# One stream of expert gathers instead of closed rounds, in a one-core encoder step

## The reference

```
a = rmsnorm(h, norm_mix);  z = a @ w_in
o_a, conv_state, S = gdn_mixer(...)      # causal conv, chunked delta rule; carries conv_state and S to the next tile
o_b, k, v, logf   = fox_mixer(...)       # causal attention over all keys so far
h = h + concat(o_a, o_b) @ w_out
h = h + peer(rmsnorm(h, norm_ffn))       # below
gate = sigmoid(rmsnorm(h, norm_ple) @ w_ple_gate)
h = h + (p @ w_ple_proj) * gate
y = rmsnorm(h, norm_final)

peer(x), per token: 8 heads pick 16 of 16384 experts each (product keys, top-16), 128 picks in all
  e, gate = picks and softmax of their scores
  a   = sum_d peer_u[e] * x              # 128 rows of 1024 gathered from peer_u
  out = sum_k gate * gelu(a) * peer_v[e] # 128 rows of 1024 gathered from peer_v
```

## Time and profile before

| | us |
|---|---|
| median of 3 runs | 4261.04 (4250.48 to 4262.46) |
| profiled execution, its own time | 4246.57 |
| its span | 4244.8 |
| DVE busy | 3223.5 (76%) |
| PE busy | 2874.7 (68%) |
| POOL busy (issuing gathers) | 2510.8 (59%) |
| ACT busy | 812.4 (19%) |

### The profile page before, as it was taken

The page is one execution under the profiler, slowest core; times in us unless marked ns, Lnnn a source line. Parts: engine busy times, 40 slices in busy tenths (PEclk is TensorE's granted clock), DMA queues, the critical chain, the costliest instruction groups (busy, mean ns, idle before and its releaser), DMA issues. The chain is left out here.

```text
span 4244.8 us, 38975 instructions
## 1 busy us (share of the span) xinstructions
PE 2874.7 (68%) x12714; PEld 1947.2 (46%) x12714; DVE 3223.5 (76%) x6384; ACT 812.4 (19%) x1609; POOL 2510.8 (59%) x2213
## 2 busy tenths in 40 slices
PE   6746576875777666766687577877688575756456
PEld 5644353643454344544365345545455434535122
DVE  3477878788877878797878887797868785796764
ACT  2112111221122112321122112221122112211111
POOL 0036765577556755676556756676556654675573
PEclk9878788987889788988899798888898787978778
DMA  5269998999999998999899999999898999999896
GB/s 187 88 252 367 335 378 310 409 364 367 358 369 387 339 395 330 405 353 376 318 409 357 362 364 356 369 343 391 334 411 307 370 345 269 389 350 374 277 388 250
DMA packets 388057, 1454.11 MB, mean 343 GB/s; under 512 B 64528, under 2 KB 67537, under 8 KB 353297
## 3 DMA queue, kind: packets, MB, share of 16 engines
q0 software_dynamic: 313344, 1140.99, 72.1%
q1 hardware_dynamic: 73200, 305.92, 18.6%
q10 hardware_dynamic: 1312, 4.72, 0.3%
HBM read 1441.69 MB, written 9.51 MB: 342 GB/s over the span
## 5 line engine op out<-in xcount | busy, mean ns | idle before, releaser
L487 POOL DMA_INDIRECT ring<-peer_u,idx_c x1061 | 1250.8, 1179 | 764.9 <-DVE dots L1412 393.7
L1000 PE MATMUL bank<-ring,diag 128*128 128x512 f32 x1920 | 1151.1, 738 | 763.5 <-DMA ring<-peer_v,idx_c 699.1
L1412 DVE CUSTOM_DVE_ANT_0 ring<-ring,xn_c 128x1024 f32<-128x1024 f32 x1088 | 1317.0, 1225 | 461.0 <-DMA ring<-peer_u,idx_c 425.4
L487 POOL DMA_INDIRECT ring<-peer_v,idx_c x1088 | 1218.0, 1120 | 666.8 <-PE bank L1000 285.2
L1000 PEld LDWEIGHTS bank<-ring,diag 128*128 128x128 f32 x1920 | 407.0, 229 | 1286.1 <-DMA ring<-peer_v,idx_c 865.3
L1420 DVE SCALAR_TENSOR_TENSOR h_c<-ring,wgt,h_c 128x1024 f32<-128x1024 f32 x608 | 781.6, 1286 | 224.0 <-DMA ring<-peer_v,idx_c 213.1
L764 PEld LDWEIGHTS bank<-aT,wring 128*128 128x128 f32 x4608 | 564.2, 202 | 113.3 <-issue 39.2
L764 PE MATMUL bank<-aT,wring 128*128 128x128 f32 x4608 | 570.4, 286 | 62.2 <-DVE aT L1036 24.5
L768 PE MATMUL bank<-wring,aT 128*128 128x256 f32 (+1 forms) x1440 | 349.1, 400 | 44.7 <-DVEq L1060 27.3
L768 PEld LDWEIGHTS bank<-wring,aT 128*128 128x128 f32 x1440 | 287.3, 202 | 122.8 <-issue 67.7
L720 ACT ACTIVATE diag<-ident,wgt 128x128 f32<-128x128 f32 x480 | 179.0, 393 | 300.1 <-PE bank L1000 234.0
(11 more groups left out here) (272 smaller groups left out, 2949.8 us busy)
## 6 DMA issues: line engine op xcount, KB each, us to landing
wring<-piece_wq SPq DMA_DIRECT2D x72, 1024.0 KB, 8.3
wring<-piece_conv_in SPq DMA_DIRECT2D x54, 1024.0 KB, 9.1
wring<-piece_out SPq DMA_DIRECT2D x36, 1024.0 KB, 8.2
wring<-piece_gate SPq DMA_DIRECT2D x36, 1024.0 KB, 8.2
wring<-piece_fox_k SPq DMA_DIRECT2D x18, 1024.0 KB, 8.2
wring<-piece_fox_q SPq DMA_DIRECT2D x18, 1024.0 KB, 8.0
ring<-peer_v,idx_c POOLq DMA_INDIRECT x1088, 6.6
ring<-peer_u,idx_c POOLq DMA_INDIRECT x1061, 7.2
```

What stands on the lines that cost most here:

```text
L487: pool.indirect_dma_start(out=ring[0:rows, n % RING, :], out_offset=None, in_=t["peer_" + kind], in_offset=bass.IndirectOffsetOnAxis(ap=id ...
L1000: last = pe.matmul(YB[g][0:peer, :], diag[0:peer, m % DIAGS, 0:peer], ring[0:peer, r, 512 * g:512 * g + 512], start=(m == 0), stop=(m == l ...
L1412: v.tensor_tensor_reduce(out=row, in0=row, in1=xn_c[0:peer, :], scale=1.0, scalar=0.0, op0=ALU.mult, op1=ALU.add, accum_out=dots[0:peer, k ...
```

## The change

All rounds stand in one block, without barriers, and the semaphores count on over the whole program (`add`, `due`, `settled`). The gathers of all tiles form one `Stream`: tile t's u stand in stream slots 68t to 68t+63 and its v in 68t+9 to 68t+72. A round has SLOTS = 68 slots instead of 73, so the last five v slots of a tile (10 gathers v) are the first five slots of the next round, mixed with the next tile's first 10 gathers u. The first u of a tile waits for that tile's `gate_done` on POOL. AHEAD, the clearing of the ring and the copies are gone; an, idx, gate and h are doubled and change roles by round parity. x is copied into the next h by ACT behind the ffn norm (`parked`), and the next tile's x is then loaded at piece wq3. p is loaded behind the first three pieces. tail_norm moves from slots 0 to 2 to slots 5 to 7. SP stores keys, values, log decays, and in the sample's round S and the conv state too, behind piece wq0 instead of behind the last piece.

```diff
-AHEAD = 3
+SLOTS = PICKS // PER_SLOT + 4
+ROUNDS = TILES + 3
...
+class Stream:
+    def __init__(self, picks, first):
...
+        for tile, count in enumerate(picks):
+            for k in range(count):
+                s = first * tile + k // PER_SLOT
+                self.slots[s].append((k % PER_SLOT, 0, tile, k))
+                self.slots[s + LAG].append((k % PER_SLOT, 1, tile, k))
...
+STREAM = Stream([PICKS] * TILES + [PICKS // 2], SLOTS)
...
+        def settled(eng, *names):
+            for name in names:
+                if base[name]:
+                    eng.wait_ge(S[name], base[name])
...
+            @block.sync
+            def _(sp):
+                if f_sample:
+                    settled(sp, "xn_ready", "s_ready")
+                    for j in range(CW - 1):
+                        sp.dma_start(out["conv_prompt"][0, 0, j].rearrange("(b p) -> p b", p=P), zT[:, :, j],
...
+                    sp.wait_ge(*due("stored", 16 * CW))
...
+                for n, name in enumerate(names):
+                    if n == WRING and has_tail:
+                        settled(sp, "gate_done", "pT_tr")
+                        sp.dma_start(prow[0:t_rows, :], t_p).then_inc(*add("p_loaded", 16))
+                    if piece0 + n >= WRING:
+                        sp.wait_ge(S["proj_done"], piece0 + n - WRING + 1)
+                        load_piece(sp, piece0 + n, name, w_loaded[(piece0 + n) % WRING])
+                    if name == "wq0":
+                        store_keys()
+                    if name == "wq3" and following is not None:
+                        load_following()
...
-                        pool.wait_ge(S["gate_done"], 1)
-                        for n, (kind, k) in enumerate(FULL.flat[:AHEAD]):
-                            if peer:
-                                pool.wait_ge(consumed[n], 2 * sched.picks // RING)
-                            gather(n, kind, k, P, idx_n, S["ahead_landed"])
-                        pool.wait_ge(S["ahead_landed"], 16 * AHEAD)
...
-                        for n in range(2 * sched.picks - RING, 2 * sched.picks):
-                            pool.wait_ge(consumed[n % RING], n // RING + 1)
...
+                    for kind, tile, k in STREAM.slots[steps[s]] if s < len(steps) else ():
+                        n = STREAM.number[kind, tile, k]
+                        if (kind, k) == ("u", 0):
+                            pool.wait_ge(S["gate_done"], tile + 1)
+                        if n >= RING:
+                            pool.wait_ge(consumed[n % RING], n // RING)
+                        gather(n, kind, tile, k)
...
                     rms(x[:], P, 4, tmp, "rms_ffn")
+                    act.activation(mix[0:f_rows, :], x[0:f_rows, :], ACT.Copy).then_inc(*add("parked", 1))
...
-            nc.all_engine_barrier(sems_to_clear=range(numbers[0], numbers[-1] + 1))
...
+        with nc.Block() as block:
+            for r in range(ROUNDS):
+                steps = range(SLOTS * (r - 1), min(SLOTS * r, len(STREAM.slots))) if r and r <= TILES + 1 else ()
+                body(block, r, [FIRST_PLAN] if r == 0 else PLAN, ...)
+        nc.all_engine_barrier(sems_to_clear=range(numbers[0], numbers[-1] + 1))
...
-    spread("tail_norm", 0, 1, 2)
+    spread("tail_pT", 3, 4)
+    s = LAG - SLOTS + PICKS // PER_SLOT
+    spread("tail_norm", s, s + 1, s + 2)
```

More of the change, by code:

```diff
@@ L357, in _ @@
                 for c in range(2):
[L358 removed]
+                    last = pe.transpose(SB[0][:, c * KEYS:(c + 1) * KEYS], xn2[0][:, c * P:(c + 1) * P], ident[:])
                 last.then_inc(S["setup_pe"], 1)
         nc.all_engine_barrier(sems_to_clear=range(numbers[0], numbers[-1] + 1))
[L363 to L369 removed]
+        pieces = [0]
@@ L370, in body @@
+        out_names = ("out_even", "out_odd")
+        chains = {}
+        def body(block, r, plan, front=None, following=None, tail=None, steps=(), blocks=TILES):
+            base.update(count)
             order = dict.fromkeys(name for slot in plan for name in slot if name in PIECES)
-            names = [name for name in order if (tail if name in TAIL_PIECES else front)]
-            assert names[:WRING] == list(first)[:WRING]
+            names = [name for name in order if (tail is not None if name in TAIL_PIECES else front is not None)]
+            assert len(names) % 2 == 0
@@ L381, in body @@
-            if tail:
-                t_i, t_rows, t_sample = tail
-                t_p = t["p_sample"][0, 0] if t_sample else t["p_prompt"][0, 0][bass.ds(t_i * P, P), :]
-                t_y = out["y_sample"][0] if t_sample else out["y_prompt"][0][bass.ds(t_i * P, P), :]
-            n_store = [0]
+            keys = blocks * P
+            an = tmp = xn2[r % 2]
+            h2 = mix = hs[r % 2]
+            idx_n, gate_n = idx2[r % 2], gate2[r % 2]
+            has_front, has_tail = front is not None, tail is not None
@@ new lines, in body @@
+            f_sample, t_sample = front == TILES, tail == TILES
+            rows_of = lambda i: DEC if i == TILES else P
+            x_of = lambda i: t["x_sample"][0] if i == TILES else t["x_prompt"][0][bass.ds(i * P, P), :]
+            if has_front:
+                f_i, f_rows = front, rows_of(front)
+                f_blk = 1 if f_sample else front
+                f_key = bass.ds(f_blk * P, P)
+            if has_tail:
+                t_rows = rows_of(tail)
+                t_p = t["p_sample"][0, 0] if t_sample else t["p_prompt"][0, 0][bass.ds(tail * P, P), :]
+                t_y = out["y_sample"][0] if t_sample else out["y_prompt"][0][bass.ds(tail * P, P), :]
@@ L413, in next_part @@
                 def next_part(name):
-                    if name not in stages or not (tail if name in TAIL_STAGES else front):
+                    if name not in stages or not (has_tail if name in TAIL_STAGES else has_front):
                         return
@@ new lines, in _, with gather, fox_keys @@
+            @block.gpsimd
+            def _(pool):
+                def gather(n, kind, tile, k):
+                    pool.indirect_dma_start(
+                        out=ring[:, n % RING, :], out_offset=None, in_=t["peer_" + kind],
+                        in_offset=bass.IndirectOffsetOnAxis(ap=idx2[tile % 2][:, k:k + 1], axis=0),
+                    ).then_inc(landed[n % RING], 16)
+                def fox_keys():
+                    settled(pool, "gate_done")
+                    pool.iota(cm[:, 0:keys], pattern=[[1, keys]], base=0, channel_multiplier=-1,
+                              allow_small_or_imprecise_dtypes=True).then_inc(*add("cm_iota", 1))
+                stages = dict(fox_keys=fox_keys)
+                next_part = walker(stages)
+                for s in range(len(plan)):
+                    for name in plan[s]:
+                        next_part(name)
+                    for kind, tile, k in STREAM.slots[steps[s]] if s < len(steps) else ():
+                        n = STREAM.number[kind, tile, k]
+                        if (kind, k) == ("u", 0):
[3 more added lines that the diff above has]
+                        gather(n, kind, tile, k)
+                if r == ROUNDS - 1:
+                    for n in range(len(STREAM.flat) - RING, len(STREAM.flat)):
+                        pool.wait_ge(consumed[n % RING], n // RING + 1)
+                    pool.dma_reset(range(landed[0].num, landed[-1].num + 1))
@@ L1484, in first_plan @@
             plan += [f"scores{g}", f"halves{2 * g}", f"halves{2 * g + 1}", f"pairs{g}"]
-    return plan + ["pick_gate"] * 6 + ["hand_rows"]
+    return plan + ["pick_gate"] * 5
 def make_plan():
-    plan = [[] for _ in range(FULL.slots)]
+    plan = [[] for _ in range(SLOTS)]
     def at(slot, *names):
```

1868 lines of the change are left out of this document (908 added, 960 removed).

## The result

| | before | after |
|---|---|---|
| median of 20 runs, us | 4249.1 (4236.9 to 4262.5) | 4271.2 (4251.0 to 4294.7) |
| ratio of the runs | 1 | 1.0053, 95% interval 1.0038 to 1.0068 |
| profiled span, us | 4244.8 | 4288.4 |

The changed kernel is slower by 0.53%, some 22 us; the forecast was 39 us faster. The 4222 us of the forecast were added to a median of three runs, 4261.0; the median of the twenty is 12 us lower, and the difference of 39 does not hang on it. Its profiled execution is one of its slowest (4290.1), so I compare stretches, each over all rounds, and sizes from medians where a run isolates them.

What follows compares the result with a forecast made beforehand. DMA engines are nearly full within a round, so only their empty time can be won. Terms -16 - 6 - 20 + 4 - 1 = -39 us, from the three-run median 4261.0 to 4222; range 4188 to 4256.

Steps and rivals of the forecast that it cites:

- eight inner boundaries: From v117 to the next tile's u10: barrier goes, gate_done wait comes, 39.5 us against 41.8; -16 us, bounds +17 and -32.
- tail_norm five slots later: Slots 5 to 7: lies beside gathers, gate0 reads its result in slot 11; counted at nothing.
- start of round 8: Sample's state chain starts in round 7, so the 23.6 us wait goes; -20 us, bounds -36 and -8.
- first boundary: End of round 0: u3 follows u2 without waiting behind the barrier; -6 us, bounds -4 and -9.
- end of round 8: Sample's conv stores ahead of wq1 may make that piece late for PE; +4 us, bounds 0 and +12.
- last boundary: After the final copy of h, ACT's norm no longer starts behind the barrier; -1.3 us, taken as -1.
- The slower rival: POOL's gate_done wait empties the queue, restart runs at 1.50 us per gather; +14 in sum, 4275 us; chance 0.08.
- its other half (wq1 late, stores hiding badly): Slower rival's terms at round 8: wq1 late by 12 us, start of round 8 gaining only 8.
- The forecast's bound of -32: Eight inner boundaries: twice the gain at each, if earlier conv_in also removes DVE's waits in slots 5 to 9.
- moved and not removed: Start of round 8: POOL's 12.6 us wait is the conv-state storing itself, whose cost stays elsewhere.
- The 4 us of that sum for the small loads: Start of round 8: small-element loads of the sample's conv state still cost some 4 us of DMA time.
- Its signs: Wrong if v117 to u10 is over 42 us, POOL's wait well over 14, or the sample's round above 490.

Runs made afterwards that it cites:

- the second profile: The changed kernel run once more, unaltered, as the yardstick beside the experiments: 4277.0 us, ratio 1.0064 to the kernel before.
- the two kernels of 73 slots: The changed kernel with rounds of 73 slots instead of 68: tail_norm in slots 5 to 7, 4206.6 us; in 0 to 2, 4173.4 us.
- the run that undoes it: 73 slots, tail_norm in 0 to 2, with SP's prompt stores and sample loads waiting for gate_done behind three weight pieces: 4196.1 us, against 4173 without.
- the run with the first tile's list: The changed kernel, every tile's gathers using a copy of the first tile's row numbers, so later u0 need not wait for gate_done: 4229.1 us, ratio 0.9945.

## Why the prediction was wrong

Point by point, forecast and measured:

| term | forecast, us | measured, us | from |
|---|---|---|---|
| eight inner boundaries | -16 | +13 | 8 x (43.4 - 41.7); in the second profile +20 |
| tail_norm five slots later | 0 | +33 to +45 | the two kernels of 73 slots; the kernel before with this alone |
| start of round 8 | -20 | -23 to -28 | by the medians of the run that undoes it; 100.7 against 137.0 in slots 5 to 19, tail_norm back in place, less 8 that round 7 pays |
| first boundary | -6 | -4 | u0 to u10 16.1 against 20.2 |
| end of round 8 | +4 | 0 | PE waited 0.32 for wq1; v60 to v117 201.8 against 202.7 |
| last boundary | -1 | -1 | ACT's norm at 4252.63, the copy's end at 4252.60 |
| sum | -39 | +13 to +30 | the whole: +22 (16 to 29 by the interval) |

**The step that failed** is the sentence "tail_norm five slots later lies beside gathers, and gate0 reads its result in slot 11", at nothing. I had asked who reads the result, and not what stands ahead of it and behind it on its engines. In slots 5 to 7 DVE's scaling stands behind conv0's work, and PE, which takes its list in order, holds conv_in3, and with it conv0 and the dots, behind the transposes. That cost 45 us in the kernel before and 33 with 73 slots, more than any other term. Two readings that lie near are not it. The late input, finished in slot 5 by the overlapping stream, is the smaller part: with the input ready PE waits 5.4 us and u10 to v20 takes 106.2 us, with the late one 9.2 us on average and 109.5 (9.6 and 108.2 in the second profile). And the length of the wait is not the price: with 73 slots and tail_norm in 0 to 2 PE waits at these transposes too, 5.0 to 6.3 us in each of rounds 2 to 7, against 5.4 in 5 to 7, and that kernel is 33 us faster. There norm_mix's transposes stand behind them in PE's list, and the first projection comes only in slot 3. The trace of before had the evidence, though I had not asked for it: POOL's longest sum of waits for another engine is for the dots, 425 us, so a stretch in which DVE stands still has no room.

**The boundaries** had the mechanism right and a size wrong. gate_done came 13.4 us behind v117 as forecast; the restart was taken at 1.28 us per gather and ran at 1.49. Not even a stream that never stopped goes at 1.28 here: without the wait (the run with the first tile's list) the 21 issues from v117 to u10 take 36.2 us, 1.72 each. I had the 1.50 in the text, as the pace right behind a barrier at the same place, and set it aside for a pace from the end of the stream, where neither norm_mix, nor conv_in, nor the dots of a new tile run beside. The slower rival said +17 for this and +13 came; its other half (wq1 late, stores hiding badly) didn't come, and its total of 4275 lies near the result by tail_norm's 45 us, which it did not have. Its reason, PE at half clock, fits the granted clock, 0.70 as a mean from v117 to u10, but with 73 slots it is 0.69 over the same gathers, which take 35 us, so the clock is not what tells them apart. What does is that POOL is held for 13 us with the DMA share at 0.30.

The forecast's bound of -32 took the boundary to be worth more if everything were ready. That part was too timid: with the gate early it is worth 8 x 6.5 = 52 us, and I had not seen it because I counted the barrier as the loss. A boundary with a barrier took 41.7 us, one without a barrier but with the gate right before its use 47.7, and that kernel is no faster than the one before (0.9992) though it has the gain at the start of round 8: where the list is finished counts for more (47.7 against 35.2) than whether a barrier stands there (41.7 against 35.2).

**The start of round 8** was right in kind, and nearly in size. Both waits went, 36 us, the 12.6 too, which I had kept as moved and not removed. But round 7, where the stores now go out, pays: it is 18.5 us longer than before, where rounds 2 to 6 are 10.5 longer on average (19.5 and 9.1 in the second profile). So 8 to 10 us were moved, and the net of 23 to 28 lies near the forecast's 20. The 4 us of that sum for the small loads no run shows by themselves. Windows of the kernel after, ahead of the conv stores and over them:

```profile
3447.00:3474.00 27.00, 23.27 (x131) 16.95 (x131) 20.10 (x81) 4.62 (x10) 14.04 (x14) 0.94 1.02 386
3474.80:3489.30 14.50, 13.94 (x86) 10.59 (x85) 12.68 (x58) 2.74 (x8) 8.55 (x8) 1.00 1.04 278
```

278 GB/s instead of 386 over 14.5 us is worth some 4 us of gathers, where the earlier trace rows had 38 GB/s and a wait of 12.6; the longest wait of POOL from 3445 to 3506 is 3.4 us. The Trainium skill says that the DMA engines take turns between queues packet by packet (DMA: Bandwidth & Descriptors, Queues, rings and completion order). This place agrees with it; the earlier trace rows did not.

**Its signs.** I had named as refuting: v117 to u10 over 42 (it was 43.4), POOL's wait well over 14 (it was 12.7), and the sample's round above 490 (it was 483). The first was met. Nothing in my list looked at slots 5 to 19 of the ordinary rounds, where most of the loss was.

## What to carry to other kernels

When a step is moved in an in-order engine's list, ask two things besides who reads its result: what stands ahead of each link of its chain at the new place (here conv0's work ahead of the scaling on DVE), and what stands behind it. A wait in front of a crowded stretch was paid by everything behind it, through PE, DVE and the ring to the DMA engines; one of the same length in slots 0 to 2 left the kernel 33 us faster.

Where a prefetch queue depends on a computed index list, removing the barrier pays only where the list is finished some slots before its first use: here two slots of lead were worth some 45 us at the boundaries, in a version that gained 73 in all, and closer packing of the tiles was worth nothing (70 and 73 slots are level with tail_norm in 5 to 7, 72 and 73 with it early). And a pace for a restart is taken from a restart under the same neighbours, not from the quietest place in the trace.

## What the runs showed of the hardware

A wait of the gathers' issuer at u0 was paid for the larger part, short or long: with 4.3 us the boundary took 3.2 us more than without one, with 12.7 us 8.8 more (both against 73 slots with tail_norm in 5 to 7), and with 15.1 us 12.5 more (against 73 slots with tail_norm in 0 to 2). In the changed kernel the DMA share was 0.30 over such a wait.

PE's wait is paid a second time in the work behind it. Windows over the 32 matmuls of conv_in3, behind PE's idle 8.1 us in the kernel after, and behind busy PE with tail_norm last in its slots:

```profile
1217.70:1223.40 5.70, 5.70 (x36) 5.70 (x35) 1.71 (x4) 0.00 (x0) 2.05 (x3) 0.65 0.90 320
```

```profile
1183.80:1187.70 3.90, 3.88 (x34) 3.88 (x35) 3.07 (x6) 3.56 (x7) 1.67 (x1) 1.00 1.00 419
```

The granted clock is 0.65, a mean between its two levels, 1.00 and 0.50 (which it shows from 701 to 710 in the same kernel), against 1.00, and the same matmuls take 5.63 us instead of 3.84. Behind the idle 5.4 us with 73 slots and in the kernel before with tail_norm moved they take 4.73 and 4.77, at 0.78 and 0.77.

The storing of single elements (three columns of conv state) held the gathers for 12.6 and 13.8 us when it began at a round's start, and for at most 3.4 us when the same stores went out beside the last wq pieces. What makes the difference was not tried.
